# Latent attention's gate as seven block products per pair of heads

## The chip, the cores and the metric

The kernel runs on one core of a Trainium2 chip. The metric is the device time of one execution in microseconds (us), the median of several runs. The core has five engines that work side by side: TensorE (PE) multiplies matrices and writes into eight PSUM banks of 512 fp32 columns, VectorE (DVE) and ScalarE (ACT) read banks and SBUF, GpSimd (POOL) reads SBUF only, and SyncE (SP) issues most of the loads. Each engine runs its own instructions in order and waits on semaphores for the others.

## What is computed

The reference runs three blocks on 512 tokens of width 1024: a retention layer, a layer of multi-head latent attention, and a block of pooling and neighbourhood attention with a feed-forward layer. The change touches the second one:

```python
def _mla_layer(x, w_in, q_norm, w_uq, w_out, k_nope, k_rope, v):
    b, s, _ = x.shape
    hproj = x @ w_in
    q_lat, gate = hproj[..., :Q_LORA], hproj[..., Q_LORA:]
    q = (_rms_norm(q_lat, q_norm) @ w_uq).reshape(b, s, H_B, QK_NOPE + QK_ROPE)
    q_nope = q[..., :QK_NOPE]
    q_rope = _rope(q[..., QK_NOPE:], ROPE_BASE_B)
    o = _causal_block_attention(q_nope, q_rope, k_nope, k_rope, v).reshape(b, s, WIDTH_B)
    return (o * jax.nn.silu(gate)) @ w_out
```

There are 16 heads of width 128, so the gate is a product of x (512 x 1024) with 1024 x 2048 weights: 256 columns of weights for two heads.

## The kernel before

Every fp32 product is made of three products of rounded numbers: an operand is split into a rounded part (hi) and its remainder (lo), and hi x hi, hi x lo and lo x hi are added up in a bank (`split_dots`, L631 to L633). The weights of a product lie in panels in HBM. SyncE loads a panel into one of two stages (`load`, L640), ScalarE writes its rounded half panels (`split_hi`, L1637), GpSimd the remainders (`split_lo`, L804), and TensorE waits for `w_lo`. A stage takes its next panel when the remainder of the one before is made. Panels of even number use one stage and one pair of buffers, those of odd number the other.

The latent layer runs over eight pairs of heads. A pair takes three panels: p with the query weights (2304 columns), p+1 with those of keys and values (2048), p+2 with those of the gate (2048). TensorE's order within a pair is written out by hand:

1. queries, 54 matmuls into banks 6, 4 and 5 (`tiles`)
2. keys, 24 matmuls of 512 columns into banks 0 and 1, and values, 48 of 256 columns into banks 2 and 3
3. scores of head 0 into banks 4 to 7 (`scores(0)`)
4. the gate of head 0: `gate_product(0, i)`, 24 matmuls of 512 columns into bank 0
5. `turn(0)`, ten transposes of the probabilities, into banks 1 to 3, then `scores(1)`
6. half of the gate of head 1 (12 matmuls), `attend(0)`, `turn(1)`, the other half, `attend(1)`

ScalarE copies the rounded parts of queries, keys and values out of the banks, makes the exponentials (`exps`), rounds the next panels and makes the gate's tanh. VectorE rotates the queries (`rotate`, L2876 on, its last step L2883), makes the remainders (L2317), the softmax (`softmax(e)`: masked maxima at L2950, scaling of the rows at L2960), the gate's (tanh + 1) x value (`gates`, L2970) and the final product with the attention's output (`gated`, L2976). GpSimd makes the remainders of the panels and, between them, issues additions in HBM (`up_sum`, `sum_step`) for later products that are already done with seven instead of eight block products; ScalarE issues the copies that these need (`copy_blocks`).

`turn(0)` waits for the scaled rows of softmax(0) one by one (m_p), as `turn(1)` does for those of softmax(1). Ahead of the pairs stand the products with x for the latents (panels B0 to B0+4, the last one M0-1), the normalised latents c and q, and the rotary key; behind them the output product BO in seven block products, whose first rounded operand comes from ScalarE (`operand_hi`) and its remainder from VectorE (`operand_lo`). The operand x for all these products lies in `xhi` and `xlo`; `xres` keeps it for the residual.

## Time and profile before

| | |
|---|---|
| median of 3 runs | 1378.1 us (1377.26 to 1378.14) |
| profiled execution | 1378.76 us, span 1376.7 us |
| TensorE busy | 1359.8 us, 99% |
| VectorE busy | 1010.8 us, 73% |
| ScalarE busy | 745.6 us, 54% |
| GpSimd busy | 306.1 us, 22% |
| the latent layer's eight pairs | 442 to 812 us of the span |

The profile is of one execution. Busy time is the sum of an engine's instructions; those of TensorE are pipelined, so the spacing of their starts, not their own duration, tells what one costs. Behind an instruction, square brackets give the idle time of its engine before it and what ended it. Where a list merges equal instructions, the second column is the time from the first one's start to the last one's end.

### The profile page before, as it was taken

The numbers are of one execution on the slowest core, as the hardware profiler recorded it, in microseconds if no ns is written. First come the engines' busy times: TensorE is split into PE (matmuls) and PEld (weight loads), VectorE is DVE, ScalarE is ACT, GpSimd is POOL, SyncE is SP. The second block draws the span as 40 slices with busy tenths as digits, with TensorE's granted clock in tenths as the row PEclk, the third lists the DMA queues.
The fourth block names the chain that finished last, engine by engine and source line by source line (L and its number), as shares of the span: only waits on it lengthen the run. The fifth ranks groups of instructions, "written<-read, shape, count | busy, mean of one in ns | idle before, by whom it ended". The sixth has DMA issues, their size and how long they took to land.

```text
span 1376.7 us, 19133 instructions
## 1 busy us (share of the span) xinstructions
PE 1359.8 (99%) x7308; PEld 1174.4 (85%) x7308; DVE 1010.8 (73%) x1671; ACT 745.6 (54%) x1197; POOL 306.1 (22%) x161
## 2 busy tenths in 40 slices
PE   8999999999999999999999999999999999999998
PEld 6788888888888888888888888878888999988887
DVE  7979787889933755454545479946877888889895
ACT  5453535457545534443444356658965666676554
POOL 2051414110043433433344210025304000000000
PEclk9999999999999999999999999999999999999999
DMA  7458575385367988966796558363122576455552
GB/s 269 164 180 225 194 206 186 127 281 206 134 186 216 312 216 238 296 171 167 212 300 161 153 212 305 123 202 124 67 85 77 162 206 169 149 181 214 196 190 103
DMA packets 53898, 260.37 MB, mean 189 GB/s; under 512 B 5568, under 2 KB 10304, under 8 KB 28224
## 3 DMA queue, kind: packets, MB, share of 16 engines
q1 hardware_dynamic: 37152, 163.04, 33.9%
q0 software_dynamic: 5760, 41.95, 15.5%
q10 hardware_dynamic: 10912, 54.40, 11.2%
q8 instruction: 46, 0.75, 0.2%
q14 instruction: 28, 0.23, 0.0%
HBM read 252.03 MB, written 91.23 MB: 249 GB/s over the span
## 4 chain that ended last, share of the span: by engine, by line
PE 82%; DVE 11%; DMA 2%; ACT 2%; issue 1%; POOL 1%; SPq 0%; DVEq 0%; ACTq 0%; POOLq 0%
PE bank L631 22%; PE bank L632 22%; PE bank L633 22%; PE bank L1362 6%; PE bank L1424 3%; PE bank L1313 3%; DVE wlo L2317 2%; PE bank L1341 1%; DMA stage<-in_w 1%; DMA v_spill<-v_tok 1%; DMA cols<-in_cols 1%; DVE wlo_a L2317 1%; DVE ar_lo L2317 1%; DVE xres L2495 1%; PE bank L1504 1%
## 5 line engine op out<-in xcount | busy, mean ns | idle before, releaser
L810 POOL TENSOR_TENSOR wlo<-stage,whi 128x1024 fp32r<-128x1024 f32 (+2 forms) x68 | 169.8, 2529 | 428.8 <-ACT whi L1644 342.5
L1647 ACT ACTIVATE whi<-stage 128x1024 fp32r<-128x1024 f32 (+2 forms) x155 | 148.2, 1002 | 104.2 <-PE bank L633 92.2
L2317 DVE TENSOR_TENSOR wlo<-stage,whi 128x1024 fp32r<-128x1024 f32 (+1 forms) x133 | 152.8, 1178 | 9.8 <-ACT whi L1647 9.8
L631 PE MATMUL bank<-xhi,whi 128*128 128x256 f32 (+1 forms) x300 | 98.4, 328 | 2.2 <-POOL wlo L946 1.2
L632 PE MATMUL bank<-xlo,whi 128*128 128x256 f32 (+1 forms) x300 | 98.1, 327 | 0.0
L633 PE MATMUL bank<-xhi,wlo 128*128 128x256 f32 (+1 forms) x300 | 98.0, 327 | 0.0
L1644 ACT ACTIVATE whi<-stage 128x1024 fp32r<-128x1024 f32 (+2 forms) x74 | 76.1, 1079 | 19.5 <-issue 14.3
L631 PE MATMUL bank<-whi,xhi 128*128 128x512 f32 (+1 forms) x204 | 78.3, 384 | 2.1 <-DVE wlo L2317 1.3
L633 PE MATMUL bank<-whi,xlo 128*128 128x512 f32 (+1 forms) x204 | 77.3, 379 | 0.0
L632 PE MATMUL bank<-wlo,xhi 128*128 128x512 f32 (+1 forms) x204 | 77.2, 378 | 0.0
L631 PEld LDWEIGHTS bank<-xhi,whi 128*128 128x128 f32 x300 | 57.0, 190 | 7.8 <-DVE hid L2527 1.4
L632 PEld LDWEIGHTS bank<-xlo,whi 128*128 128x128 f32 x300 | 57.1, 190 | 5.0
L633 PEld LDWEIGHTS bank<-xhi,wlo 128*128 128x128 f32 x300 | 57.1, 190 | 5.0
L1647 ACT ACTIVATE whi<-oT 128x1024 fp32r<-128x1024 f32 x34 | 34.1, 1053 | 38.8 <-DVE oT L2778 17.9
L859 POOL TENSOR_TENSOR wlo<-stage,whi 128x1024 fp32r<-128x1024 f32 x12 | 30.1, 2528 | 106.4 <-ACT whi L1647 106.4
L2317 DVE TENSOR_TENSOR pt_lo<-bank,pt_hi 128x384 fp32r<-128x384 f32 (+1 forms) x48 | 26.6, 596 | 35.3 <-ACT pt_hi L1647 35.3
L1362 PE MATMUL bank<-xhi,whi 128*128 128x512 f32 x128 | 50.7, 396 | 0.0
L1362 PE MATMUL bank<-xhi,wlo 128*128 128x512 f32 x128 | 50.0, 391 | 0.0
L1362 PE MATMUL bank<-xlo,whi 128*128 128x512 f32 x128 | 49.9, 390 | 0.0
L631 PEld LDWEIGHTS bank<-whi,xhi 128*128 128x128 f32 x204 | 38.3, 188 | 10.1 <-DVE wlo L2317 1.7
L631 PE MATMUL bank<-ql_hi,whi 128*128 128x512 f32 x120 | 46.9, 391 | 0.0
L632 PE MATMUL bank<-ql_lo,whi 128*128 128x512 f32 x120 | 46.7, 389 | 0.0
(501 smaller groups left out, 4365.2 us busy)
## 6 DMA issues: line engine op xcount, KB each, us to landing
stage<-in_w SPq DMA_DIRECT2D x71, 1024.0 KB, 4.9
tsum<-in_w ACTq DMA_DIRECT2D x32, 1024.0 KB, 12.8
stage<-tsum SPq DMA_DIRECT2D x32, 1024.0 KB, 4.8
tsum<-in_w POOLq DMA_DIRECT2D x16, 1024.0 KB, 9.9
tsum<-tsum POOLq DMA_DIRECT2D x16, 1024.0 KB, 9.9
stage<-in_w SPq DMA_DIRECT2D x8, 1152.0 KB, 6.3
usum<-in_w POOLq DMA_DIRECT2D x8, 1024.0 KB, 10.0
stage<-usum SPq DMA_DIRECT2D x32, 256.0 KB, 4.1
```

The costliest lines, as they stand in the source:

```text
L631: pe.matmul(dst, a_hi, b_hi, start=start, stop=False, skip_group_check=onto)
L632: pe.matmul(dst, a_hi, b_lo, start=False, stop=False, skip_group_check=onto)
L633: return pe.matmul(dst, a_lo, b_hi, start=False, stop=stop, skip_group_check=onto)
L810: pool.tensor_tensor(lo[:, to], stage[p % 2][:, r], hi[:, to].bitcast(F32), ALU.subtract).then_inc(w_lo, 1)
L859: pool.tensor_tensor(lo[:, r], a_staged(h, j)[:, r], hi[:, r].bitcast(F32), ALU.subtract).then_inc(g_plo, 1)
L1313: last = pe.matmul(bank[4 + q][:, 0:w], left, right, start=i == 0, stop=i == 4)
L1341: last = pe.transpose(dst[min(kt, 2)][:, at:at + P], prob[:, src:src + P], ident[:, :])
L1362: last = pe.matmul(bank[0][:, :], left[:, k, f], right[:, k, :], start=i == 0, stop=i == 23)
L1424: last = pe.matmul(bank[m][:, :], left[:, k, m * P:(m + 1) * P], right[:, k, :], start=i == 0, stop=i == 23)
L1644: act.activation(parts(p)[0][:, to], stage[p % 2][:, r], ACT.Copy).then_inc(w_hi, 1)
L1647: act.activation(dst, src, ACT.Copy, scale=scale).then_inc(signal, 1)
L2317: dve.tensor_tensor(dst, src, hi.bitcast(F32), ALU.subtract).then_inc(signal, 1)
```

## The change

The gate of a pair is W^T x, with W of 1024 x 256 and x of 1024 x 512. W and x are cut into four blocks each: W into a11, a21, a12, a22 of 512 x 128 (k by features), x into b11, b21, b12, b22 of 512 x 256 (k by tokens). Seven products of sums of blocks give the whole (Winograd's form), each with 4 k steps x 3 matmuls of 256 columns: 84 matmuls of 256 in place of 48 of 512.

- Sums of x (t1 to t4) are made once, ahead of the pairs: eight additions on VectorE into `xsum`, ScalarE's rounded parts, VectorE's and (for t4) GpSimd's remainders. t1 and t2 take a free place, t3 lies over `xres`, whose rows 0 to 2 go to HBM (`x_spill`, issued on ScalarE's queue ahead of `wkr` and `mask`) and come back behind the pairs; t4 overwrites b12.
- Sums of W are made in each pair: three by VectorE in the stage of panel p+2 (`first_sums`), between the remainders of keys and values, and the fourth by GpSimd (`fourth_sum`) in the stage of panel p+3, ahead of the remainder of the second half of p+2.
- The gate's weights take two panels, p+2 (three blocks loaded, four used) and p+3 (two loaded, three used), so a pair has four panels and 1536 more columns to split.
- The products go into halves of banks 1, 0 and 5. ScalarE keeps bank 1 in `gate_kept`, VectorE adds up (`add_up`, five times), tanh and gates are in three pieces.
- The next pair's query panel is rounded in two halves, the first after exps(1), the second after the tanh of head 0; before it was both halves after exps(0). The copies of `copy_blocks(DN, ...)` are issued two or three to a pair instead of eight at once. The first weight panel and operand of BO stand where the next panel would.

```diff
+                    def first_sums():
+                        dve.wait_ge(landed[p % 2], 8 * n + LANDED[p % 2] + 16 * ((p + 2 - B0) // 2 + 1))
+                        dve.tensor_tensor(slot(near, G_S1), slot(near, G_S3), slot(near, G_S1), ADD).then_inc(m_ws, 1)
+                        dve.wait_ge(m_ws, c(4, USED + 1))
+                        dve.tensor_tensor(slot(near, G_S2), slot(near, G_S1), slot(near, G_A11), SUB).then_inc(m_ws, 1)
+                        dve.tensor_tensor(slot(near, G_S3), slot(near, G_A11), slot(near, G_S3), SUB).then_inc(m_ws, 1)
...
                     for m in range(2):
                         dve.wait_ge(m_kvhi, c(4, m + 1))
                         lo_of(kn_lo[:, m, :], bank[m][:, :], kn_hi[:, m, :], m_kvlo)
+                    first_sums()
                     for m in range(2):
...
                     softmax(0)
-                    turned(0, 0)
-                    gates(0)
-                    turned(0, 1)
-                    turned(0, 2)
+                    dve.wait_ge(m_k, c(1, USED + 1))
+                    dve.wait_ge(m_g, c(4, 6))
+                    add_up(0)
+                    dve.wait_ge(m_u, c(5, USED + 1))
+                    add_up(1)
+                    dve.wait_ge(m_u, c(5, USED + 2))
+                    add_up(2)
+                    for b in range(3):
+                        turned(0, b)
                     softmax(1)
-                    gated(0, bank[1])
                     for b in range(3):
                         turned(1, b)
+                    dve.wait_ge(m_g, c(4, 7))
+                    add_up(3)
+                    gates(0, 0, first_t, bank[0][:, first_t])
+                    gates(1, 0, second_t, kept[0])
+                    gated(0, bank[1])
+                    dve.wait_ge(m_g, c(4, 8))
+                    add_up(4)
                     if last and s == 1:
                         operand_lo(BO, 0)
-                    gates(1)
+                    gates(2, 1, slice(0, SEQ), gate_kept[:, HALF:])
                     gated(1, bank[7])
```

On TensorE and GpSimd:

```diff
                     scores(0)
-                    for i in range(24):
-                        gate_product(0, i)
+                    gate_block(x_t2, p + 2, G_S2, 0, bank[1][:, first_t])
+                    gate_block(x_t3, p + 2, G_S3, 0, bank[1][:, second_t]).then_inc(m_g, 1)
+                    gate_block(x_b11, p + 2, G_A11, 1, bank[0][:, first_t])
+                    gate_block(x_t1, p + 2, G_S1, 1, bank[0][:, second_t], True).then_inc(m_g, 1)
...
                     scores(1)
-                    pe.wait_ge(m_gt, c(2, 3))
-                    for i in range(12):
-                        gate_product(1, i)
+                    pe.wait_ge(m_u, c(5, USED + 3))
+                    gate_block(x_b21, p + 3, G_A12, 0, bank[0][:, first_t], True)
                     attend(0, bank[1])
                     for i in range(10):
                         turn(1, i)
-                    for i in range(12, 24):
-                        gate_product(1, i)
+                    gate_block(x_b22, p + 3, G_S4, 0, bank[0][:, second_t], True).then_inc(m_g, 1)
+                    pe.wait_ge(t_l, USED + 4)
+                    gate_block(x_t4, p + 3, G_A22, 1, bank[5][:, first_t]).then_inc(m_g, 1)
                     attend(1, bank[7])
...
+            def fourth_sum(pair):
+
+                p = M0 + 4 * pair + 3
+                near, far = (stage[(M0 + k) % 2] for k in (0, 1))
+                to, x, y, op = slot(far, G_S4), slot(far, G_A12), slot(near, G_S2), SUB
+                pool.wait_ge(landed[p % 2], LANDED[p % 2] + 16 * ((p - B0) // 2 + 1))
+                pool.wait_ge(m_ws, USED + 4 * pair + 2)
+                pool.tensor_tensor(to, x, y, op).then_inc(m_ws, 1)
```

On ScalarE, ahead of the pairs and within one:

```diff
             act.wait_ge(n_x, TT)
+            act.dma_start(t["x_spill"], xres[:, 0:3, :]).then_inc(aux["x"], 16)
             act.dma_start(wkr[:, :], t["wkr"]).then_inc(aux["kr"], 16)
...
             split_hi(B0 + 3, b_c, TT)
+            act.wait_ge(aux["x"], 32)
+            for i, x in enumerate((x_t3, x_t1, x_t2)):
+                act.wait_ge(t_s, USED + i + 1)
+                copy(x[0], xsum[:, (2, 0, 1)[i]], t_h)
             for j in range(KC):
...
                     exps(0)
...
-                        split_hi(p + 3, m_kv, c(4, 4), PANEL, n)
-                    turned(0, 0)
-                    tanh(0)
-                    turned(0, 1)
-                    turned(0, 2)
+                    act.wait_ge(m_g, c(4, 5))
+                    act.wait_ge(m_gt, c(3, 3))
+                    copy(gate_kept[:, 0:SEQ], bank[1][:, :], m_k)
+                    act.wait_ge(m_ws, c(4, USED + 4))
+                    split_hi(p + 3, m_kv, c(4, 4), PAN, n)
...
+                    for b in range(3):
+                        turned(0, b)
                     exps(1)
+                    next_hi(0)
                     for b in range(3):
                         turned(1, b)
+                    act.wait_ge(m_u, c(5, USED + 4))
+                    tanh(0, first_t, bank[0][:, first_t])
+                    tanh(0, second_t, gate_kept[:, 0:HALF])
+                    next_hi(1)
...
+                    act.wait_ge(m_u, c(5, USED + 5))
+                    tanh(1, slice(0, SEQ), gate_kept[:, HALF:])
```

## Rows read from the trace of the kernel before

**Rows 1.** The page: TensorE's busy time; the chain that ended last, by engine.
```profile
PE 1359.8 (99%) x7308; PEld 1174.4 (85%) x7308; DVE 1010.8 (73%) x1671; ACT 745.6 (54%) x1197; POOL 306.1 (22%) x161
...
PE 82%; DVE 11%; DMA 2%; ACT 2%; issue 1%; POOL 1%; SPq 0%; DVEq 0%; ACTq 0%; POOLq 0%
```
**Rows 2.** Busy time by stretch; columns: stretch, length, engines' busy us, clock, DMA share, GB/s.
```profile
442.00:466.00 24.00, 23.65 (x127) 20.09 (x126) 21.29 (x29) 10.20 (x17) 8.26 (x4) 1.00 0.97 294
...
673.70:719.90 46.20, 46.20 (x257) 40.51 (x255) 24.83 (x66) 20.25 (x40) 17.36 (x10) 1.00 0.99 314
```
**Rows 3.** The chain in order of time: start, length, what (gate products).
```profile
700.18 5.46 PE bank L1362 x24
...
709.71 2.75 PE bank L1362 x12
...
746.39 5.46 PE bank L1362 x24
```
**Rows 4.** TensorE in order of time: first and last of 48 matmuls of the values.
```profile
506.55 0.28 PE L631 MATMUL bank<-whi,c_hi 128*128 128x256 f32 x1
...
512.08 0.28 PE L633 MATMUL bank<-whi,c_lo 128*128 128x256 f32 x1
```
**Rows 5.** GpSimd and ScalarE in order of time, one pair: panels and an HBM addition.
```profile
678.38 4.78 POOL L810 TENSOR_TENSOR wlo<-stage,whi 128x1024 fp32r<-128x1024 f32 x2 [15.92 <-ACT whi L1644]
...
702.61 5.31 POOL L810 TENSOR_TENSOR wlo<-stage,whi 128x1152 fp32r<-128x1152 f32 x2 [1.14 <-ACT whi L1644]
716.03 0.82 POOL L818 DMA_DIRECT2D tsum<-in_w  x1 [8.11 <-DMA tsum<-in_w]
...
701.36 2.22 ACT L1644 ACTIVATE whi<-stage 128x1152 fp32r<-128x1152 f32 x2
```
**Rows 6.** The first pair: ScalarE's and TensorE's instructions in order of time.
```profile
462.58 2.01 ACT L1644 ACTIVATE whi<-stage 128x1024 fp32r<-128x1024 f32 x2
...
466.56 1.28 ACT L2008 ACT_TABLE_LOAD   x1
...
465.86 0.73 PE L1313 MATMUL bank<-kn,qn_hi 128*128 128x512 f32 x2 [0.35 <-DVE kn L2317]
```
**Rows 7.** VectorE beside GpSimd, in order of time, at 92 and at 496 us.
```profile
92.05 0.68 DVE L2651 TENSOR_TENSOR work<-bank,rope_a 128x512 f32<-128x512 f32 x1
92.05 5.23 POOL L859 TENSOR_TENSOR wlo<-stage,whi 128x1024 fp32r<-128x1024 f32 x2 [9.35 <-ACT whi L1647]
...
93.36 1.66 DVE L2654 TENSOR_TENSOR work<-work 128x512 f32<-128x512 f32 x1
94.95 2.88 DVE L2655 TENSOR_TENSOR work<-work 128x512 f32<-128x512 f32 x1
...
496.75 4.88 DVE L2883 TENSOR_TENSOR grow<-grow 128x512 f32<-128x512 f32 x1
```
**Rows 8.** Head 1 in a pair: softmax's first and last instruction, and the transposes.
```profile
708.89 0.69 DVE L2950 CUSTOM_DVE_ANT_0 bank<-bank,mask 128x512 f32<-128x512 f32 x1
...
712.65 0.35 DVE L2960 TENSOR_SCALAR prob<-prob,sm 128x256 f32<-128x256 f32 x1
...
714.15 1.28 PE L1341 MATMUL bank<-ident,prob 128*128 128x128 f32 x10
```
**Rows 9.** DMA issues: what, engine, count, KB each, median us to landing.
```profile
stage<-in_w SPq DMA_DIRECT2D x71, 1024.0 KB, 4.9
...
v_spill<-v_tok ACTq DMA_DIRECT2D x1, 1024.0 KB, 10.6
```
**Rows 10.** Ahead of the pairs: VectorE's remainders of c; TensorE's third product begins.
```profile
412.82 2.73 DVE L2320 SCALAR_TENSOR_TENSOR c_lo<-bank,cols,c_hi 128x512 fp32r<-128x512 f32 x4 [10.77 <-ACT c_hi L1647]
...
424.04 0.30 PE L631 MATMUL bank<-whi,xhi 128*128 128x320 f32 x1
```
**Rows 11.** Behind the pairs: the operand's remainder and the product that reads it.
```profile
809.58 1.23 DVE L2317 TENSOR_TENSOR br_lo<-bT,br_hi 128x1024 fp32r<-128x1024 f32 x1
...
812.30 0.44 PE L631 MATMUL bank<-whi,br_hi 128*128 128x512 f32 x1
```

More of the change, by code:

```diff
@@ L61 @@
 M0 = B0 + 5
-L0 = M0 + 3 * PAIRS
+L0 = M0 + 4 * PAIRS
 WO = L0 + 8
@@ L807, in split_lo @@
                     pool.wait_ge(w_hi, 2 * n + (MORE + 2 * p + s + 1))
+                    if s == 1 and M0 <= p < L0 and (p - M0) % 4 == 2:
+                        fourth_sum((p - M0) // 4)
+                        pool.wait_ge(m_ws, USED + (p - M0) + 2)
                     r, to = half_at(p, s, width)
@@ L1353, in attend, with gate_block @@
                         last.then_inc(m_o, 1)
-                    def gate_product(m, i):
-                        wh, wl = panel(p + 2, KX)
-                        k, f = i // 3, slice(m * P, (m + 1) * P)
-                        if m == 0 and i % 3 == 0:
-                            need(p + 2, n, KX, k)
-                        left, right = ((wh, xhi), (wh, xlo), (wl, xhi))[i % 3]
-                        last = pe.matmul(bank[0][:, :], left[:, k, f], right[:, k, :], start=i == 0, stop=i == 23)
-                        if i == 23:
-                            last.then_inc(m_g, 1)
+                    def gate_block(x, panel_, k, late, dst, onto=False):
+                        wh, wl = [slot(w[:, LINE:], k).rearrange("p (k n) -> p k n", k=PK) for w in parts(panel_)]
+                        pe.wait_ge(w_lo, 2 * n + (2 * panel_ + 1 + late))
+                        for kk in range(PK):
+                            last = split_dots(pe, dst, wh[:, kk, :], wl[:, kk, :], x[0][:, kk, :], x[1][:, kk, :],
+                                              kk == 0 and not onto, kk == PK - 1, onto)
+                        return last
                     pe.wait_ge(b_krlo, 4)
@@ L1636, in _, with split_hi @@
         def _(act):
-            def split_hi(p, used=None, count=0, width=PAN, n=0):
+            def split_hi(p, used=None, count=0, width=PAN, n=0, halves=(0, 1)):
                 act.wait_ge(landed[p % 2], 8 * n + LANDED[p % 2] + 16 * ((p - B0) // 2 + 1))
@@ L1641, in split_hi @@
                     act.wait_ge(used, count)
-                for s in range(2):
+                for s in halves:
                     r, to = half_at(p, s, width)
@@ L1656, in operand_hi, with weights_hi @@
                 copy(operand_parts(st, d)[0], operand(st, d), d_shi)
-            def weights_hi(st, d):
+            def weights_hi(st, d, halves=(0, 1)):
                 act.wait_ge(d_ld[(st.at + d) % 3], loads(st.at + d))
-                for b in range(2):
+                for b in halves:
                     r = slice(b * PAN // 2, (b + 1) * PAN // 2)
@@ L3233, in panels, with gate_panels @@
     return x.reshape(-1, P, nk * width)
+def gate_panels(w):
+    a11, a21, a12, a22 = (panels(w[k:k + 512, f:f + P], PK, P) for k in (0, 512) for f in (0, P))
+    return np.concatenate([a22, a21, a11, a22], 2), np.concatenate([a22, a12], 2)
 def kernel(**inputs):
```

174 lines of the change are left out of this document (127 added, 47 removed).

## Prediction

> **What bounds the kernel now.** First the page: TensorE is busy for 99% of the span, its clock is granted in full throughout, and the chain that ended last runs for 82% over it [rows 1]. Next the table by stretch: in a pair of heads TensorE has no gap, while VectorE is busy for 24.8 us of 46.2, ScalarE for 20.3 and GpSimd for 17.4 [rows 2]. The chain in order of time gives the period: the same gate product begins at 700.18 and 746.39, so a pair takes 46.21 us [rows 3]. So a matmul taken away counts in full, provided that whatever TensorE waits for is ready earlier too; the rest of the reading asks that of every new wait. The first pair is tighter: there TensorE waits 0.35 us for VectorE's kn at 465.86 [rows 6], with the DMA engines 97% busy [rows 2].
>
> **The gain.** A pair's gate is 48 matmuls of 512 columns now: 5.46 + 2.75 + 2.75 = 10.96 us [rows 3] (the third piece is like the second). Afterwards it is 7 blocks x 4 k x 3 = 84 matmuls of 256 columns. The value product has just that form: 48 of them, the first at 506.55, the last at 512.08, so 0.1177 us each [rows 4]. 84 x 0.1177 = 9.89 us. Gain 1.07 us a pair, **8.6 us** for eight.
>
> **What is added, per pair.** ScalarE and GpSimd split 2304 + 2048 + 2048 + 1536 columns instead of 2304 + 2048 + 2048. GpSimd takes 2.39 us per 1024 columns (4.77 for two) and 2.66 per 1152 [rows 5], so 1536 more and the fourth sum of 512 cost it 4.8 us; it has 29 us free. VectorE gets three sums of 512 columns (0.69 each, taking L2883 where nothing holds it up), and five additions of 256 to 512 less its old form. These are totals and hide nothing; what matters is the order.
>
> I count from the start of a pair (673.7 in the trace). Key product 12.3 to 17.7, value product to 23.4, scores to 26.3, as now. VectorE ends kn_lo at 19.2, the three sums at 21.3; ScalarE, between the two value copies, rounds panel p+2 by 22.4 and 23.4 (2.01 us for two halves [rows 5]); GpSimd's first half is there at 24.9, needed at 26.3. Fourth sum until 26.1, second half until 28.5, needed two blocks (2.83 us) later at 29.1. **Covered, by 1.4 and 0.6 us; price nothing** as long as GpSimd is not held up.
>
> **The lock.** What turns the order into a price is seen in rows 7: a VectorE instruction whose inputs all lie in SBUF doesn't run beside a GpSimd tensor instruction. GpSimd's two take 5.23 us from 92.05, the first until some 94.5. L2654, 0.69 on its own by L2651's form, takes 1.66 and ends 0.5 after that first one; L2655 then sits through the second (2.88); at 496.75 L2883, also 0.69 alone, misses the boundary between two GpSimd instructions and takes 4.88. VectorE instructions that read a bank are not affected (L2651 at 92.05 beside GpSimd's first: 0.68). The Trainium skill ("SBUF — State Buffer", section "SBUF: two separate sides") says that VectorE and GpSimd share a port pair as an exclusive lock for a whole instruction, with the loser blocked; the trace agrees, and it is the rule that speaks against this change, which adds work on both sides.
>
> Where it bites in a steady pair: GpSimd begins panel p+3 at 31.0 (ScalarE keeps the bank at 29.4 to 29.9, then rounds) and holds until 33.4. The second addition (kept onto kept, SBUF only) is due at 32.6, so it runs at the boundary, until 33.7. Behind it on VectorE are the third addition, three pt_lo (1.62 in all) and softmax(1), which begins at 35.65 instead of 35.2. In the trace softmax takes from 708.89 to the end of the last scaling at 713.00, 4.1 us [rows 8]: it ends at 39.8. TensorE, for its part, comes earlier: turn 31.95, scores to 36.05, one gate block of 1.41 instead of 2.75 us, attention 1.86, so it wants the four scaled rows at 39.3 to 39.6. The slack of 1.5 us that stands there now (713.00 against 714.15 plus 0.3) [rows 8] becomes **a stall of 0.2 us**; bounds 0 (sooner by 0.3) and 1.4 (the boundary missed, as at 496.75, with the half panel of 1.2 us).
>
> End of the pair, T being the end of turn(1): the gate's block of T + 1.6, add_up 0.4, two tanh, half of the next panel (1.16), GpSimd 2.66: T + 6.8. Before, this panel was rounded right after exps(0) at 701.36 and done 12 us before it was needed [rows 5]. TensorE ends the pair at T + 4.7 and needs the second half at its tenth matmul, 2.05 later: T + 6.75. **0.1 us a pair**; 0 to 0.6. Together 7 x 0.3 = 2.1 us.
>
> **The first pair.** VectorE is behind there by its chain for the rotary key, so that TensorE waits for kn [rows 6]. Without panel p+2 in front (ScalarE 462.58 to 464.59 [rows 6]) kn_lo ends at 464.8, so the wait of 0.35 goes. The sums end at 466.7, ScalarE's half at 467.8, GpSimd's at 470.3; TensorE wants it at 468.35: 2.0 us. Second half 474.0, wanted at 473.2: 0.8. VectorE's softmax comes after the second value remainder at 470.0 and a table load of 1.28 us [rows 6]; its scalings are SBUF-only and meet GpSimd's second half, the remainder of the fourth operand (queued behind panel p+2, 2.4 us) and panel p+3, one scaling for each boundary: the last at 478 to 480, against 476.9. 2 us (bounds 0 and 3.5). softmax(1) likewise, 1 (0 and 2). Sum 5.8 less 0.35, **5.5 us**; 2.5 to 8.
>
> **Ahead of the pairs.** The spill of 1.5 MB is queued ahead of wkr and mask on ScalarE's DMA queue. A 1 MB panel takes 4.9 [rows 9], so some 6: ScalarE goes on 4 us later, c_tok and after it panel B0+3 with it. By the same counting TensorE comes to their last half 1.8 us after they are ready: covered. Eight sums and three remainders of 128x1024 at 1.22 us (1.14 in series) on VectorE, with two of GpSimd's instructions between: 403.2 to 420.9, where VectorE idles for 10.8 us today, up to c_lo at 412.82 [rows 10]. ScalarE waits for the second and third sum (413.8, 415.0) with the copies of c_hi and the panel of the third product behind it; that panel's second half is done by GpSimd at 426.1, wanted 1.3 after the product's start at 424.04 [rows 10]: **0.8 us**; bounds 0 and, if the spill lands as late as the 10.6 us of v_spill [rows 9], 4.
>
> **Behind the pairs.** The next product needs the rounded operand's remainder from VectorE. It is made at 809.58 now, 2.7 us before TensorE comes to it at 812.30 [rows 11]. In the change ScalarE rounds it only after the second half of the first weight panel and is done at T + 5.0, and GpSimd splits that panel from T + 4.1 to T + 6.5: the remainder, SBUF-only, ends at T + 7.6 against T + 4.7. **2.9 us**; bounds 0 (it gets in first) and 5 (three more loads now queue behind panel p+3). The reload of the spilled rows has 20 us before its first reader: nothing.
>
> **Sum.** -8.6 + 2.1 + 5.5 + 0.8 + 2.9 = +2.7 us. The profiled execution took 1378.8 us (span 1376.7), the median of the runs is 1378.1: the profiled one becomes 1381.5, the median **1380.8**. Gain and stalls nearly cancel: a known gain in each pair against one-off losses around them.
>
> **Rivals.**
> - **The covers hold: faster.** Each one-off at its low end: 2.5 + 0 + 0, and 1 for the pairs: -8.6 + 3.5 = -5.1, **1373.0**. For it: the low ends only need VectorE to reach the lock first, and GpSimd does wait for a closed series of VectorE instructions in places. Against it: the first pair's chain of sum, rounding, remainder has no slack at all. 25%.
> - **The boundary is missed: slower.** The place is the second addition and softmax(1) behind it in pairs 2 to 8. If VectorE doesn't get in between GpSimd's two instructions, each pair stalls 1.2 more, +8.4: **1389**. It decides as soon as the addition ends more than 0.3 us later than at 33.7. For it the case at 496.75, against it L2654 [rows 7]. 17%.
> - **GpSimd is late for the gate: slower.** It issues additions in HBM between panels and waits for earlier copies (8.11 us idle before the issue at 716.03 [rows 5]). If such a wait ends after 31 us, the fourth panel comes late: 1 us in six pairs, and 2 more in the first, **1388**. 8%.
> - **The change saves no TensorE time** because narrow matmuls are bound by their weight loads (PEld 40.5 of 46.2 us [rows 2]): then +11, **1389**. The value product speaks against it. 2%.
>
> **How the numbers follow.** The forecast (48%) covers 1376 to 1386 from the bounds of its terms. About 0.2%, 2.8 us, is what a measurement here tells from no change: 1375.3 and 1380.9. The forecast lies on the upper edge, so its 48% fall 4 to faster, 27 to no change, 17 to slower. The first rival gives 21 to faster and 4 to no change, the others 27 to slower, less 3 where smaller one-offs offset them. Faster 25%, same 34%, slower 41%. Range 1371 to 1391: it leaves out the extremes of the first two rivals.
>
> **What would show it.** Gate: 84 matmuls, 9.9 us, in the pair. Period of pairs 2 to 8: 45.4 (45.1 if nothing stalls, 46.6 if the boundary is missed). Waits of TensorE: for wlo at the first gate block of the first pair, 2 us; for prob at turn(1), 0.2; for wlo in the query product; for br_lo at the end, 3. The second addition should last until GpSimd's instruction ends. I am wrong if the period isn't within 0.3 of 45.4 or if the first pair loses less than 2.5.

## The result, and the profile after

| | before | after |
|---|---|---|
| median of the runs, us | 1378.1 (1377.3 to 1378.3, 4 runs) | 1394.8 (1394.1 to 1397.2, 4 runs) |
| profiled execution, us (its span) | 1378.8 (1376.7) | 1394.8 (1392.9) |

The ratio is 1.0126, with a 95% interval of 1.0108 to 1.0143: 16.7 us slower, where +2.7 was forecast and 1391 was the upper end of the range.

The page of the changed kernel, TensorE's busy time and the chain by engine, against [rows 1]:

```profile
PE 1359.0 (98%) x7596; PEld 1182.8 (85%) x7596; DVE 1091.8 (78%) x1754; ACT 768.5 (55%) x1233; POOL 351.2 (25%) x186
...
PE 77%; DVE 14%; DMA 3%; issue 3%; ACT 2%; POOL 1%; DVEq 0%; ACTq 0%; SPq 0%; POOLq 0%
```

TensorE lost 5 points of the chain; its busy time is the same (1359.8 before), though the gate needs 8.6 us less. So the loss is idle time, and something has eaten the gain within the busy time as well. The first matmul of some pairs, and of the stage behind them, shows where (TensorE in order of time: start, us, line, operands; in brackets the wait before it and what ended it):

```profile
441.41 0.47 PE L1028 MATMUL bank<-ql_hi,whi 128*128 128x512 f32 x1
...
497.02 0.45 PE L651 MATMUL bank<-ql_hi,whi 128*128 128x512 f32 x1
...
554.41 0.45 PE L1028 MATMUL bank<-ql_hi,whi 128*128 128x512 f32 x1
...
599.53 0.45 PE L651 MATMUL bank<-ql_hi,whi 128*128 128x512 f32 x1
...
780.57 0.45 PE L651 MATMUL bank<-ql_hi,whi 128*128 128x512 f32 x1
...
828.63 0.80 PE L651 MATMUL bank<-whi,br_hi 128*128 128x512 f32 x1 [2.53 <-DVE br_lo L2393]
```

The same places of the kernel before are 441.57, 488.81, 535.02 and then every 46.21 us, 812.30 for the last [rows 11]. So the first pair takes 55.6 us (47.2 before), **the second 57.4** (46.2), the five after it 45.2 on average (46.2), the eighth 48.1. In us against the kernel before: -0.2 ahead of the pairs, +8.4, +11.2, five times -1.0, +1.9; together +16.3, where the span grew by 16.2. TensorE's waits from 380 to 880 us (line, what ended them: us in total, times, longest):

```profile
PE bank L651 <- POOL wlo L852: 13.0, 4, 9.1
PE bank L1394 <- DVE prob L3073: 3.9, 1, 3.9
PE bank L651 <- DVE br_lo L2393: 2.5, 1, 2.5
```

And the table by stretch (stretch, length, busy us of TensorE, its weight loads, VectorE, ScalarE, GpSimd, clock, DMA share, GB/s), against [rows 2]:

```profile
466.00:488.00 22.00, 14.89 (x91) 13.41 (x90) 18.27 (x40) 10.71 (x22) 12.86 (x7) 0.84 0.92 292
...
497.02:520.00 22.98, 13.88 (x59) 10.98 (x59) 9.71 (x12) 4.81 (x7) 7.31 (x5) 0.87 0.92 261
520.00:545.00 25.00, 25.00 (x163) 23.13 (x163) 13.57 (x36) 10.02 (x20) 12.49 (x8) 0.91 0.65 158
554.41:599.54 45.13, 45.09 (x293) 41.01 (x292) 30.66 (x75) 21.25 (x43) 22.26 (x13) 1.00 0.80 230
825.00:840.00 15.00, 12.47 (x53) 10.31 (x52) 14.45 (x14) 9.36 (x12) 2.37 (x1) 0.89 0.85 327
```

The fourth of these rows is a pair without a stall: 45.13 us, TensorE busy throughout, clock 1.00. The other four hold a wait or the time right behind one, and in them the clock is under 1. The waits add up to 2.53 + 0.70 + 3.88 = 7.1 us in the first pair, 9.1 in the second and 2.5 at the end, 18.7 in all. The rest of the loss is TensorE at its lower level (1.2 GHz; the granted clock is 0.50 from 518.76 to 524.10) after a wait:

```profile
509.28 0.39 PE L653 MATMUL bank<-ql_hi,wlo 128*128 128x512 f32 x1
518.76 0.80 PE L651 MATMUL bank<-c_hi,whi 128*128 128x512 f32 x1 [9.10 <-POOL wlo L852]
519.35 0.63 PE L652 MATMUL bank<-c_lo,whi 128*128 128x512 f32 x1
519.78 0.63 PE L653 MATMUL bank<-c_hi,wlo 128*128 128x512 f32 x1
```

Matmuls of 512 columns start 0.43 us apart here until 524.0, and 0.23 apart from 524.5 on. Against 45.13 us plus the waits, the first pair is 3.4 us longer and the second 3.2; 0.7 of the 3.4 are in the kernel before too (47.24 less 46.21 less the wait of 0.35), whose first matmuls also start further apart. Behind the wait at 828.63, with the same spacing for seven matmuls, it is 7 x 0.2 = 1.4. So **the clock costs some 2.7 + 3.2 + 1.4 = 7.3 us**, and the prediction had no term for it. The first two figures are what is left over; the 13 matmuls from 518.76 to 524.45 take 5.7 us in place of 3.0, which is 2.7 of the second pair's 3.2.

### The profile page after: what moved, and what is told of

The parts are those of the page before. It is cut to its first block, busy times and chain, and to the rows that moved or that the text cites. A ratio compares the mean times of both kernels' runs of the same rounds, so it can differ in the third digit from the quotient of the medians.

```text
span 1392.9 us, 20011 instructions
## 1 busy us (share of the span) xinstructions
PE 1359.0 (98%) x7596; PEld 1182.8 (85%) x7596; DVE 1091.8 (78%) x1754; ACT 768.5 (55%) x1233; POOL 351.2 (25%) x186
## 4 chain that ended last, share of the span: by engine, by line
PE 77%; DVE 14%; DMA 3%; issue 3%; ACT 2%; POOL 1%; DVEq 0%; ACTq 0%; SPq 0%; POOLq 0%
PE bank L651 22%; PE bank L652 22%; PE bank L653 22%; PE bank L1479 3%; PE bank L1366 2%; DVE wlo L2393 2%; DMA tsum<-in_w 1%; POOL wlo L852 1%; PE bank L1394 1%; DMA v_spill<-v_tok 1%; DVE wlo_a L2393 1%; DVE xlo L2393 1%; DVE ar_lo L2393 1%; DVE xres L3086 1%; DVE xres L2571 1%
## 5 line engine op out<-in xcount | busy, mean ns | idle before, releaser
L852 POOL TENSOR_TENSOR wlo<-stage,whi 128x1024 fp32r<-128x1024 f32 (+2 forms) x84 | 203.2, 2452 | 392.4 <-ACT whi L1699 291.3
L651 PE MATMUL bank<-xhi,whi 128*128 128x256 f32 (+1 forms) x428 | 133.9, 313 | 2.5 <-POOL wlo L994 1.2
L653 PE MATMUL bank<-xhi,wlo 128*128 128x256 f32 (+1 forms) x428 | 133.0, 311 | 0.0
L652 PE MATMUL bank<-xlo,whi 128*128 128x256 f32 (+1 forms) x428 | 133.0, 311 | 0.0
L651 PEld LDWEIGHTS bank<-xhi,whi 128*128 128x128 f32 x428 | 80.5, 188 | 8.2 <-DVE hid L2603 1.4
L653 PEld LDWEIGHTS bank<-xhi,wlo 128*128 128x128 f32 x428 | 80.4, 188 | 5.0
L2072 ACT ACTIVATE prob<-bank,sm 128x512 f32<-128x512 f32 (+1 forms) x64 | 33.2, 524 | 30.3 <-DVE sm L3063 30.2
L653 PE MATMUL bank<-ql_hi,wlo 128*128 128x512 f32 x120 | 46.8, 390 | 0.0
L2393 DVE TENSOR_TENSOR wlo_a<-stage,whi_a 128x1024 fp32r<-128x1024 f32 x38 | 45.8, 1220 | 0.0
L653 PEld LDWEIGHTS bank<-whi,xlo 128*128 128x128 f32 x204 | 38.3, 188 | 7.0
```

Of the source, the lines that this page charges most:

```text
L651: pe.matmul(dst, a_hi, b_hi, start=start, stop=False, skip_group_check=onto)
L652: pe.matmul(dst, a_hi, b_lo, start=False, stop=False, skip_group_check=onto)
L653: return pe.matmul(dst, a_lo, b_hi, start=False, stop=stop, skip_group_check=onto)
L852: pool.tensor_tensor(lo[:, to], stage[p % 2][:, r], hi[:, to].bitcast(F32), ALU.subtract).then_inc(w_lo, 1)
L2072: act.activation(prob[:, at:at + w], bank[4 + q][:, 0:w], ACT.Exp, scale=-1.0, bias=sm[:, 1, 4 * e + q:4 * e + q + 1], accum_out=sm[:, 2, ...
L2393: dve.tensor_tensor(dst, src, hi.bitcast(F32), ALU.subtract).then_inc(signal, 1)
```

## Where the 9.1 us of the second pair come from

GpSimd of the changed kernel, then of the kernel before, at the same place of the second pair:

```profile
490.61 2.65 POOL L852 TENSOR_TENSOR wlo<-stage,whi 128x1152 fp32r<-128x1152 f32 x1 [9.28 <-ACT whi L1699]
496.42 2.68 POOL L852 TENSOR_TENSOR wlo<-stage,whi 128x1152 fp32r<-128x1152 f32 x1 [3.15 <-ACT whi L1699]
499.03 0.82 POOL L877 DMA_DIRECT2D usum<-in_w  x1
515.52 0.82 POOL L860 DMA_DIRECT2D tsum<-in_w  x1 [15.67 <-DMA tsum<-in_w]
516.07 4.96 POOL L852 TENSOR_TENSOR wlo<-stage,whi 128x1024 fp32r<-128x1024 f32 x2
```

```profile
487.40 0.82 POOL L835 DMA_DIRECT2D usum<-in_w  x1 [9.91 <-DMA tsum<-in_w]
495.49 0.82 POOL L818 DMA_DIRECT2D tsum<-in_w  x1 [7.27 <-issue]
496.04 5.03 POOL L810 TENSOR_TENSOR wlo<-stage,whi 128x1024 fp32r<-128x1024 f32 x2
```

Both kernels have two additions in HBM behind the remainder of the second pair's query panel, and the remainder of panel p+1 (keys and values) behind those. In both, the second is issued only when the first has landed: 8.1 us apart before (landed after 7.8), 16.5 in the changed kernel (landed after 16.2). The key product needs the first half of the remainder at its start and the second half six matmuls later. The kernel before had the halves at 498.7 and 501.07 for a key product that begins at 501.11 and reads the second half from 502.5 on: 2.4 and 1.4 us to spare. In the changed kernel the first half is there at 518.7, and TensorE starts at 518.76. The changed kernel rounds the query panel at the end of a pair and not in its middle. The additions start 11.6 us later (499.03 against 487.40); 8.2 of these are the later start of the pair and 3.4 the later place within it. These 3.4 and the 8.4 by which the second addition comes later behind the first, less the 2.4 to spare, make 9.4, where the wait measures 9.1. The DMA issues from 497 to 515 us (what, queue, count, KB each, median us to landing):

```profile
tsum<-in_w ACTq DMA_DIRECT2D x3, 1024.0 KB, 12.1
usum<-in_w POOLq DMA_DIRECT2D x1, 1024.0 KB, 16.2
stage<-in_w SPq DMA_DIRECT2D x1, 768.0 KB, 15.7
o_spill<-gt SPq DMA_DIRECT2D x2, 256.0 KB, 16.6
```

The label of the wait names tsum, but those copies only land in the same stretch. The program has GpSimd wait there for earlier copies alone, issued up to 447.2, and these had landed: no transfer is under way in the stretch ahead.

```profile
488.00:497.02 9.02, 9.02 (x73) 8.76 (x72) 6.28 (x21) 5.47 (x12) 3.26 (x2) 1.00 0.00 1
```

Three edits tell apart the place in the queue, the number of additions and the copies.

**One addition fewer in that place.**

```diff
-                if 3 <= m < 11:
-                    sum_step(BO, m - 3, (28, 28), 16)
-                elif 11 <= m < 23:
-                    sum_step(DN, m - 11, (36, 44), 24)
+                if 4 <= m < 12:
+                    sum_step(BO, m - 4, (28, 28), 16)
+                elif 12 <= m < 24:
+                    sum_step(DN, m - 12, (36, 44), 24)
```

> The changed kernel with one edit in GpSimd's queue: behind panel p+1 of the second pair only one addition through HBM is issued (usum) and not two; the 20 additions of tsum that follow each come one panel later. Theory: TensorE's wait of 9.1 us in the second pair (for the remainder of panel p+1, 516.1 to 521.0) stems from GpSimd's second addition, which was issued 16.5 us after the first, when the first had landed, with the panel's remainder queued behind it. Then the wait goes, and with it the half-speed stretch behind it: the second pair takes 45.2 to 46.5 us in place of 57.4, and the kernel 1383.5 to 1386. Rival: the panel itself or the transfers of that stretch are late, whatever GpSimd does: the second pair stays at 55 to 58 us and the kernel at 1394 to 1396.

1384.95 us (1.0062, 1.0045 to 1.0079), 9.9 less than the changed kernel. GpSimd of this run in order of time, and its second pair in the table by stretch:

```profile
498.95 0.82 POOL L877 DMA_DIRECT2D usum<-in_w  x1
499.82 4.80 POOL L852 TENSOR_TENSOR wlo<-stage,whi 128x1024 fp32r<-128x1024 f32 x2
515.32 0.82 POOL L860 DMA_DIRECT2D tsum<-in_w  x1 [10.70 <-DMA tsum<-in_w]
```

```profile
496.96:542.29 45.33, 45.27 (x292) 41.12 (x292) 30.64 (x75) 21.43 (x43) 22.47 (x13) 1.00 0.79 230
```

The addition behind usum still waits until 515.3, now with nothing urgent behind it, and both the stall and the half-speed stretch are gone. The panel had landed: the remainder runs at 499.8.

**The same additions, one of them earlier.** The last addition of usum moves from behind the query panel of the second pair to behind panel p+3 of the first.

```diff
+                if k == 3:
+                    up_sum(1, 3)
                 if k % 4 == 3:
                     continue
                 if m < 3:
                     up_sum(1, m)
-                elif m == 3:
-                    up_sum(1, 3)
```

> The changed kernel with all its transfers, and one of GpSimd's additions earlier in its queue: the last addition of usum is issued behind panel p+3 of the first pair (about 482), where GpSimd has nothing to do until 490.6, and no longer behind the next pair's query panel (499.03); the addition of tsum stays there. The kernel before issued the pair of additions at 487.40 and 495.49, since there the next pair's query panel was rounded in the middle of a pair and not at its end. Theory: the wait of 9.1 us is the price of this place in the queue: with usum landed by 495, the addition of tsum is issued at 499 at once and the remainder of panel p+1 starts behind it at 500, so the wait goes as with one addition fewer: second pair 45.2 to 46.5 us, kernel 1383.5 to 1386. Rival: with three copies, a panel and a store under way from 497 on, any addition there holds GpSimd up: second pair 52 to 56 us, kernel 1390 to 1394.

1383.5 us (1.0047, 1.0031 to 1.0062), 11.4 less. The second pair takes 45.2 us. The first is 1.3 us shorter than in the changed kernel, which the edit need not have done: its length differs by as much between runs whose edits don't touch it (54.6 to 56.1). GpSimd of this run in order of time:

```profile
476.74 0.82 POOL L877 DMA_DIRECT2D usum<-in_w  x1
...
488.58 0.91 POOL L877 DMA_DIRECT2D usum<-in_w  x1 [7.45 <-issue]
...
498.21 0.84 POOL L860 DMA_DIRECT2D tsum<-in_w  x1
499.09 4.79 POOL L852 TENSOR_TENSOR wlo<-stage,whi 128x1024 fp32r<-128x1024 f32 x2
```

With the same transfers under way the wait goes, so the place in the queue is the cause. The addition meant for 482 went out at 488.6, 11.8 us after the one before it; the next one, 9.6 us later, did not wait at all.

**The copies as in the kernel before.** ScalarE issues eight in the third pair and eight in the sixth.

```diff
-                        if (1, 1, 1, 2, 2, 2, 3, 3, 4, 4, 4, 5, 5, 5, 6, 6)[d] == 2 * it + s:
+                        if (2, 5)[d // 8] == 2 * it + s:
```

> The changed kernel with one edit on ScalarE: the 16 copies for the last stage's weight sums are issued as in the kernel before, eight in the third pair and eight in the sixth, and none in the second. Theory: the first of GpSimd's two additions of the second pair took 16.2 us to land because three of these copies (1 MB each), a panel and a store were under way with it; without the copies it lands in about 8 us as in the kernel before, GpSimd's remainder of panel p+1 starts 8 us earlier (about 508), and TensorE waits 0.4 to 3.5 us in place of 9.1; kernel 1385 to 1390. Rival (the copies have no part in it, the two additions are slow in any case or the panel is late): the wait stays at 8 to 10 us and the kernel at 1394 to 1396.

**1414.4 us** (1.0266, 1.0248 to 1.0283), 19.6 more; neither side expected that. In the second pair the theory was half right: the additions are 12.5 us apart and not 16.5, and TensorE waits 5.1 us and not 9.1. GpSimd and TensorE of this run in order of time:

```profile
512.65 0.82 POOL L860 DMA_DIRECT2D tsum<-in_w  x1 [11.65 <-issue]
...
515.89 0.80 PE L651 MATMUL bank<-c_hi,whi 128*128 128x512 f32 x1 [5.05 <-POOL wlo L852]
```

Thus the three copies explain 4.0 of the additional 8.4 us; for the other 4.4 the panel and the store moved there are left, which I did not take apart. The third and the sixth pair, which take eight copies each, last 56.9 and 56.6 us instead of 45.2, with TensorE waits of 9.4 and 9.1 us for a remainder. With four panels a pair, eight copies in one cost over 11 us; to spread them was part of what makes the change possible.

**The copies spread, in the kernel before.**

> The kernel before with one edit on ScalarE: the 16 copies for the last stage's sums are issued as in the changed kernel, three of them in the second pair. Theory: the kernel before already had the two additions behind one another in GpSimd's queue in its second pair, and panel p+1's remainder was ready 0.04 us before TensorE needed it; with three copies of 1 MB under way the first addition lands in 10 to 14 us in place of 8.1, and TensorE waits 2 to 6 us in the second pair; kernel 1380.5 to 1387. Rival: the copies do no harm by themselves, only the changed kernel's own transfers (four panels a pair, a store beside them) do: wait under 0.5 us, kernel 1377.5 to 1379.

1377.8 us (0.9998, 0.9989 to 1.0007): the rival was right. (The 0.04 us of the expectation compare the end of both halves with the start of the product; by halves 2.4 and 1.4 us were to spare.) Its first addition goes out at 485.68, 1.5 us ahead of the copies of that pair (487.18), and lands in 8.9 us; the second follows at 494.86 and takes 15.7, so that the third waits until 510.82, where nothing is late for it. Spreading alone costs nothing here; it is the later place of the additions that puts the first of them behind the copies.

## The first pair

Three of VectorE's four scalings of head 0 in the changed kernel, and GpSimd beside them, in order of time:

```profile
472.64 2.09 DVE L3073 TENSOR_SCALAR prob<-prob,sm 128x512 f32<-128x512 f32 x1
474.83 2.24 DVE L3073 TENSOR_SCALAR prob<-prob,sm 128x128 f32<-128x128 f32 x1
477.18 4.37 DVE L3073 TENSOR_SCALAR prob<-prob,sm 128x384 f32<-128x384 f32 x1
```

```profile
472.06 2.38 POOL L852 TENSOR_TENSOR wlo<-stage,whi 128x1024 fp32r<-128x1024 f32 x1
474.40 2.59 POOL L938 TENSOR_TENSOR xlo<-xsum,xhi 128x1024 fp32r<-128x1024 f32 x1
476.93 0.82 POOL L877 DMA_DIRECT2D usum<-in_w  x1
477.51 3.82 POOL L852 TENSOR_TENSOR wlo<-stage,whi 128x1024 fp32r<-128x1024 f32 x2
```

The first two get through at the boundaries of GpSimd's instructions, as predicted. The third begins at 477.18, ahead of panel p+3, and yet ends only with that panel's second half. It misses both the start and the boundary.

**The fourth operand's remainder earlier.**

```diff
-                if k == 2:
+                if k == 1:
                     pool.wait_ge(t_h, USED + 4)
                     pool.tensor_tensor(x_t4[1], xsum[:, 3], x_t4[0].bitcast(F32), ALU.subtract).then_inc(t_l, 1)
```

> The changed kernel with one edit in GpSimd's queue: the remainder of x_t4 (2.59 us, once) stands behind panel p+1 of the first pair and no longer between the halves' work of panels p+2 and p+3, so that it runs while VectorE is not yet in its scalings. Theory: VectorE's third scaling of the first pair (4.37 us, where an undisturbed one takes about 1.2) was blocked by it, and TensorE's wait of 3.9 us at the first turn came from that; the wait falls to 0.3 to 1.5 us, and the first pair from 55.6 to 51 to 53 us; kernel 1390 to 1392.5. Rival: the chain of VectorE is late by the new sums ahead of it and by panel p+2's remainder, and the port is no more than a part: the wait falls by under 1 us and the kernel stays at 1393.5 to 1395.

1390.1 us (1.0086, 1.0069 to 1.0103), 4.7 less; the profiled execution took 1394.1, the longest of the four. The scalings after it:

```profile
475.28 2.08 DVE L3073 TENSOR_SCALAR prob<-prob,sm 128x512 f32<-128x512 f32 x1
477.46 0.29 DVE L3073 TENSOR_SCALAR prob<-prob,sm 128x128 f32<-128x128 f32 x1
477.86 0.42 DVE L3073 TENSOR_SCALAR prob<-prob,sm 128x384 f32<-128x384 f32 x1
```

The 384-column one takes 0.42 instead of 4.37 us (the 1.2 of the expectation were too many), and TensorE no longer waits for the scalings at all. The first pair takes 52.1 us (47.24 - 1.07 + 5.5 = 51.7 was forecast for it). But the moved instruction now meets a remainder of the rotary key (2.77 us where an undisturbed one takes 0.69), which makes VectorE 2.6 us late for everything behind it: TensorE waits 1.6 us for kn, new in this run, and still 2.7 at the first gate block. So GpSimd's work beside it is shown as the cause of the long scaling; this place was only half a remedy. The runs show that one engine holds up the other, not what they share. The Trainium skill ("SBUF — State Buffer", section "SBUF: two separate sides") describes the exclusive port pair and the blocked loser. The trace agrees, 4.37 against 0.42 us, and adds that a waiting VectorE instruction does not always get the boundary.

## The start of the next stage

TensorE waits 2.5 us for the remainder br_lo of the stage's first operand (826.03, 2.55 us long beside a GpSimd remainder). Two runs tried to have it earlier.

**Rounded ahead of the last gate work.**

```diff
                         turned(1, b)
+                    if last and s == 1:
+                        act.wait_ge(bld[0], 32)
+                        operand_hi(BO, 0)
                     act.wait_ge(m_u, c(5, USED + 4))
...
-                    if last and s == 1:
-                        act.wait_ge(bld[0], 32)
-                        operand_hi(BO, 0)
```

(and operand_lo(BO, 0) likewise on VectorE, ahead of add_up(3))

> The changed kernel with one edit in the last pair: the first operand of the stage after the pairs is rounded on ScalarE, and its remainder taken on VectorE, ahead of that pair's last gate work and not behind it. Theory: TensorE's wait of 2.5 us at the start of the stage is for this remainder, which a GpSimd remainder held up at the shared port; with it taken earlier the wait goes (0 to 0.4 us), and the seven matmuls at half speed behind it too; kernel 1390.5 to 1392.5. Rival: the operand's load has not landed earlier, or the weights' remainder on GpSimd (to 827.5) ends the wait as well: 1 us or less is won and the last pair's tail gets longer; kernel 1393.8 to 1396.

1396.4 us (1.0139, 1.0122 to 1.0156): nothing won. The last pair does get 2.5 us shorter (45.6), but the next stage then waits 1.8 us for VectorE's remainder of the second weights and 1.4 for GpSimd's of the first.

**The operand's load earlier as well.** Its load stood behind that of the second weights, whose buffer the fourth panel now holds until 815.5.

```diff
             seven_load(BO, 0)
+            sp.wait_ge(m_kv, 4 * PAIRS)
+            heads_load(0)
             sp.wait_ge(m_g, 4 * PAIRS + 2)
             sp.dma_start(xres[:, 0:2, :], t["x_spill"][:, 0:2, :]).then_inc(aux["x"], 16)
             sp.wait_ge(w_lo, 2 * L0)
             seven_load(BO, 1)
```

> The changed kernel with the two things the first operand of the stage after the pairs needs, both earlier: its load from HBM is issued by SyncE before it waits for the last weight panel's remainder (about 800 in place of 815.5), and, as in the run before, its rounding and its remainder come ahead of the last gate work. Theory: the load, queued behind the load of the next weights, whose buffer the fourth panel holds until 815.5, was the late one in that run (rounded at 822.69 as soon as it had landed), so the earlier order could bring nothing alone; with both, the operand is ready by about 822 and TensorE's wait at the start of the stage falls from 2.5 us to 0.5 or less, with no further wait of over 1 us behind it; kernel 1389.5 to 1392. Rival: the wait moves on to the next operand and to the weights' remainder (1.8 and 1.4 us in the run before): kernel 1393.5 to 1396.5.

1394.5 us (1.0124, 1.011 to 1.0139). The last pair takes 45.3 us, without any stall, and the stage behind has lost 2.4 us by its second product and 4.1 by 12.3 us after its start. The rival was right: the wait moves on.

## The edits together

**Four together:** one addition fewer in the second pair, the fourth operand's remainder on GpSimd where VectorE reads only from PSUM (behind the rotary key's remainders: `pool.wait_ge(b_krlo, 4)` ahead of it at k == 1), and the two edits of the section above.

> The changed kernel with four edits together: GpSimd's second addition of the second pair one panel later; x_t4's remainder on GpSimd while VectorE is in the rotation's products from PSUM (behind the rotary key's remainders, before panel p+2); the heads' load early; the first operand's rounding ahead of the last gate work. Theory: the three stalls are apart and their prices add: 9.9 (second pair), about 5 to 5.5 (first pair, with the clock behind it), 3 to 4.5 (start of the next stage) off 1394.8: kernel 1375 to 1378, the first pair 50 to 51 us, the others 45.1 to 45.4. Rival: the first pair's wait for the gate blocks' weights and its turn hang on the new sums and not on the port, so the first pair stays at 52 to 54 us: kernel 1378 to 1381.

1382.2 us (1.0025, 1.0015 to 1.0034), above both. The first pair takes 49.7 us, a little less than the theory said: the waits for the third gate block and the scalings are gone, the one for the first gate block is still 2.2. But the 2.6 us by which the pairs end ahead of the kernel before (809.67) have become a lag of 2.3 by 823.3: the prices don't add. (The profiled execution was the longest of the ten, 1385.6.)

**A fifth:** the eight copies ahead of the first pair are issued behind the rounding of its panel p+1.

```diff
-            act.wait_ge(t_copy, 16 * 21)
-            copy_blocks(BO, 0, 1, 2, 3)
             for it in range(PAIRS // 2):
...
                     split_hi(p + 1, m_g, c(4, 4), PAN, n)
+                    if (it, s) == (0, 0):
+                        act.wait_ge(t_copy, 16 * 21)
+                        copy_blocks(BO, 0, 1, 2, 3)
```

> The run with four edits together, and a fifth: the eight copies for the next stage's sums, which ScalarE issues ahead of the first pair (441.1 to 447.2), come behind the rounding of panel p+1, so that GpSimd takes its remainder before VectorE comes to the end of the rotation of the rotary key (2.54 and 2.53 us there in place of 0.69 and 0.7). Theory: VectorE's chain of the first pair starts 2.5 to 3.7 us earlier, the sums of the gate's weights and panel p+2 with it, and the wait of 2.5 us at the first gate block goes: first pair 47 to 49 us, kernel 1372.5 to 1375.5. Rival: the first gate block waits for TensorE's own order and the panel's load (landed late), so that less than 1 us is won against the run with four edits.

1381.5 us (1.0023, 1.0013 to 1.0032), 6 us above the theory, though the first pair takes 47.7 us as it said and the wait at the first gate block is gone. The rival's figure, under 1 us against the four edits, came true (0.7), but not for its reason. (The second pair takes 46.9, as the second half of its query panel is 1.5 us late.) The pairs end at 808.09, **4.2 us ahead of the kernel before**, and 13 us later that lead has turned into a lag of 0.8. VectorE of this run in order of time:

```profile
810.21 1.67 DVE L3097 SCALAR_TENSOR_TENSOR gt<-gt,xres 128x512 f32<-128x512 f32 x1 [0.70 <-ACT gt L2092]
811.98 0.69 DVE L3103 TENSOR_TENSOR gt<-bank,gt 128x512 f32<-128x512 f32 x1
813.33 1.22 DVE L2400 TENSOR_TENSOR br_lo<-bT,br_hi 128x1024 fp32r<-128x1024 f32 x1 [0.66 <-ACT br_hi L1708]
814.48 1.22 DVE L2413 TENSOR_TENSOR comb<-bT 128x1024 f32<-128x1024 f32 x1
815.61 2.35 DVE L2400 TENSOR_TENSOR wlo<-stage,whi 128x1024 fp32r<-128x1024 f32 x2
```

The second product needs br_lo and the first half of wlo at 813.6 and begins at 816.98.

**The second operand and weights ahead of the last gate.** operand_hi(BO, 1) and weights_hi(BO, 1) move ahead of the last tanh on ScalarE, their remainders ahead of gates(2) on VectorE.

> The run with five edits, and the second operand and the second weights of the next stage rounded on ScalarE, and their remainders taken on VectorE, ahead of the last gate of the last pair and no longer behind it (VectorE's remainders of the second weights end at about 814 in place of 818.0, TensorE needs them from 813.5 on). Theory: the 5.0 us that the stage lost in its first 9 us was VectorE's and ScalarE's order in the last pair; it falls to 0 to 1.5: kernel 1376 to 1378.5, at or under the kernel before. Rival: VectorE has too much to do there in any order (the next operands' sums and remainders are later instead), and 3 us or more stay: kernel 1380 to 1382.

1380.9 us (1.0021, 1.0012 to 1.003). The wait for the second weights shrinks to 1.2 us, and there are others now: 0.7 for br_lo, 1.4 for wlo_a of the third. The stage has lost 1.5 us at its second product and 3.2 at its third: the rival again. **Without the two edits at the start of the stage:**

> The run with five edits without the two at the start of the next stage (heads' load and first operand's rounding as in the changed kernel). Theory: these two only moved the loss: with them the pairs ended 4 us earlier than in the kernel before, but the next stage lost 5.0 us in its first 9 us (waiting for the second operand and the second weights, of which VectorE's remainders come last, then at half the clock). Without them the last pair takes 48 to 49.3 us, with 1.4 to 1.7 us of half clock behind it: kernel 1380 to 1382.5, as with them. Rival: the early load of the heads also delayed later transfers (a wait of 1.8 and one of 1.4 us near 935 and 945 that the changed kernel has not): 2 to 4 us less, 1377.5 to 1380.

1381.9 us (1.0023, 1.0013 to 1.0032), as with them, and so as the theory said. Its profiled execution, among its fastest at 1379.4 us, adds up against the kernel before: -0.2 ahead, +0.7 and +0.8 in the first two pairs, -4.7 in the next five, +2.9 in the eighth, +2.4 of half clock behind it (twelve matmuls after a wait of 3.7 us) and -1.1 in the rest of the kernel: +0.8 us of span (1377.5 against 1376.7).

So the stalls of the first two pairs can be removed, and with them about 13 of the 16.7 us. What keeps the change from winning is the join to the next stage: the gate's last sum, its tanh and its multiplications end later in a pair than the old gate's, and in the last pair the operands of the next stage queue behind them on VectorE and ScalarE. That is read from the traces; no order that I tried gave back more than it took, so no run shows the join without its loss.

## Why the prediction was wrong

- **The gain: right.** 45.13 us for a pair without a stall against 46.21: 1.08 us, forecast 1.07. The matmuls of 256 columns are not bound by their weight loads.
- **Steady pairs: right, a little dear.** 0.1 us of stalls a pair (45.23 on average), forecast 0.3. The second addition gets the boundary: in the fourth pair it runs from 632.18 to 633.30, while GpSimd works on panel p+3 from 630.62 to 634.46; that is 33.8 us into the pair, forecast 33.7. So the rival of the missed boundary falls.
- **"End of the pair": the step that failed.** That paragraph priced the moved rounding of the next query panel at 0.1 us, for TensorE's sake, and did not go on to what stands behind that panel in GpSimd's queue: two additions, and panel p+1 behind them. Going on would have shown the additions 8.1 us apart at best (495.49 less 487.40), hence 499.0 and 507.1, and the first half of p+1's remainder ready at 510.1 for a key product at 509.5: a stall of 0.6 with nothing else under way, and transfers of three engines there. The third rival had the mechanism (an addition in HBM that waits, and GpSimd late behind it), but looked for it at the fourth panel, gave it 8% and left it out of every term. Missing: 9.1 us of wait and 3.2 of clock. The prediction's sign of being wrong, a period of pairs 2 to 8 not within 0.3 of 45.4, came up in the second pair (57.4) and the eighth (48.1); the five between keep to it.
- **The first pair: waits sized well, clock missed.** First gate block 2.53 us (forecast 2.0), third 0.70 (0.8), wait for kn gone (as forecast); the scalings 3.88 (2, bound 3.5), of which one missed boundary; softmax of head 1 none (1). Together 7.1 against 5.8, and 2.7 of clock on top.
- **Ahead of the pairs:** -0.2 us, forecast +0.8; c_lo and the third product were covered.
- **Behind the pairs:** the pair 2.9 us longer, forecast 2.9, and again 1.4 of clock behind it. The cause named was only the first of a row: taking it away brought up the second operand and the second weights.
- **The clock** was granted in full throughout the kernel before (mean 0.999), and I took from this that it would stay so. It fell after three of the four waits of 2.5 us and more in the changed kernel.

Term by term, measured less forecast: first pair 9.4 - 5.5 = +3.9 (both without the gain), second 12.3 - 0.3 = +12.0, the next five 0.5 - 1.5 = -1.0, the eighth with the stage's start 2.9 - 3.2 = -0.3, ahead of the pairs -0.2 - 0.8 = -1.0, clock behind them +1.4, and -1.6 from the rest of the kernel, which ran that much faster behind 832 us. Sum +13.4, and 16.2 - 2.7 = 13.5 is to be explained.

**Open:** the variants with several edits vary more from run to run (1378.0 to 1385.6 for the four together) than the kernel before. The profiled executions of 1385.6 and 1384.0 us lose 4 us between 885 and 945 us, which the one of 1379.4 does not; the first thing late there is the landing of v_spill, for which VectorE waits 12.7 and 12.5 us, 9.5 in the kernel before and 8.7 in the one of 1379.4. What delays it I did not find out. Nor is it known why the scaling of 477.18 did not go ahead of a GpSimd instruction that started later.

## What to carry to other kernels

When a change moves one preparation to a later place, follow the whole queue behind it up to the next thing that TensorE reads, a pair further on too; 2.4 us to spare, which nobody has to count today, are found only this way. An accumulating DMA in GpSimd's queue holds up all behind it until the one before has landed. And price a stall of TensorE above its length: here 18.7 us of waits cost some 7.3 more at half clock.

## What the runs showed of the hardware

- GpSimd issues an addition in HBM (1 MB) only when its previous one has landed. The four pairs of additions above landed after 7.8, 11.5, 12.2 and 16.2 us, depending on what else was moved, and the next one went out 8.1, 11.8, 12.5 and 16.5 us after its predecessor, though the program asks there only for copies that had landed before its wait began. Everything behind it in the queue waits as well. No addition between 380 and 850 us went out before its predecessor had landed, in either kernel.
- After waits of 2.5, 3.9 and 9.1 us TensorE ran at 1.2 GHz (0.43 us for each matmul of 512 columns in place of 0.23) until 3 to 6 us after the wait's end. After one of the waits of 2.53 us (828.63) it did, after the other (470.79) it ran at 2.4 GHz at once (0.12 for 256 columns); both follow more than 25 us without a wait, and what tells them apart is not shown. A shorter wait was enough in the run with the heads' load early: after one of 1.82 us, ended at 832.78, matmuls of 512 columns were 0.43 us apart from 833.63 to 836.6. The Trainium skill ("TensorE: Matmul & The Clock Gate", section "HAM oscillation — how this bites in real kernels") tells of a kernel whose TensorE waits for its next operand and then starts at the lower clock. The trace agrees for three of the four waits of 2.5 us and more, at a price of some 7.3 us.
- A VectorE instruction from SBUF to SBUF that GpSimd's work holds up got the boundary between two GpSimd instructions at 472.64, 474.83 and 632.18, and missed one right behind a DMA issue of GpSimd at 477.18 (4.37 us in place of 0.42).
